# The seams between the stages of a hybrid-layer kernel, and the order inside its operand block

## What is computed

```
h = rms_norm(x) * (1 + scale) + shift                 # scale, shift, gate: silu(c) @ ada_w + ada_b
p = h @ w_in                                          # gate, u (512 each), r, k, v (512 each), lora (288)
u = silu(layer_norm(causal_conv31(u * sigmoid(gate))) * g + b)            # the conv branch
decay = exp(-exp(-softplus(-(w0 + tanh(wd) @ w2)) - 0.5));  a = sigmoid(a0 + ad @ a2)
kk = k * k_k / |k * k_k| per head;  k = k * (1 + (a - 1) * k_a)
y  = wkv7_scan(r, decay, k, v, kk, a)                 # recurrence; then norm per head, bonus, gate
x  = x + gate_m * rms_norm(concat[u, y] @ w_out)
x  = x + gate_f * rms_norm(channel_mix(h2))           # up (5632 wide), conv3, silu * value, down (2816)
for i in (0, 1):                                      # two hybrid layers
    attn, ssm = window_attention(x @ w_in_2[i]), state_space(x @ w_in_2[i])
    x = layer_norm(alpha * x + concat[attn, ssm] @ w_out_2[i]) * ln_g + ln_b
```

## Time and profile before

| | |
|---|---|
| time, median of 3 runs | 3605.99 us (3601.85 to 3607.5) |
| time of the profiled execution | 3603.5 us |
| its span, first to last instruction | 3601.4 us |
| TensorE busy | 3210.5 us (89%) |
| TensorE weight loads busy | 2560.5 us (71%) |
| VectorE, ScalarE, GpSimd busy | 1544.3, 1054.2, 1141.1 us |
| mean granted clock of TensorE | 0.938 of full speed |
| operand block | 318.5 to 424.7 us of the span |
| recurrence | 424.7 to 690.8 |
| down projection | 1329.6 to 1618.2 |
| first and second hybrid layer | 1618.2 to 2616.1, 2616.1 to 3601.4 |

### The profile page before, as it was taken

How to read it: one execution, slowest core, us unless ns; L and a number is a source line. 1 busy time by engine, 2 the same in 40 slices (tenths; PEclk the granted TensorE clock), 3 DMA queues, 4 the chain that set the end, 5 groups by cost and what they waited for, 6 DMA issues and landing times. The chain is left out here.

```text
span 3601.4 us, 49506 instructions
## 1 busy us (share of the span) xinstructions
PE 3210.5 (89%) x21000; PEld 2560.5 (71%) x21016; DVE 1544.3 (43%) x2066; ACT 1054.2 (29%) x1842; POOL 1141.1 (32%) x730
## 2 busy tenths in 40 slices
PE   6998699777999989958999998879699999988795
PEld 4885389666888878747777776768577777767684
DVE  3997644434222233341244333860312443338603
ACT  3002323323222221221244343440212443435302
POOL 2442311103333323332333332233323333323333
PEclk8998699888999999989999998989899999989898
DMA  5113300222111112113121223022131212230221
GB/s 188 52 49 98 110 4 4 68 106 62 47 52 47 47 32 97 44 73 118 47 77 59 65 82 152 1 82 97 62 82 47 79 57 65 82 152 1 97 84 64
DMA packets 211747, 254.90 MB, mean 71 GB/s; under 512 B 9408, under 2 KB 164160, under 8 KB 209120
## 3 DMA queue, kind: packets, MB, share of 16 engines
q1 hardware_dynamic: 200736, 212.21, 18.2%
q10 hardware_dynamic: 10240, 37.75, 2.7%
q0 software_dynamic: 576, 2.10, 0.1%
HBM read 203.80 MB, written 46.14 MB: 69 GB/s over the span
## 5 line engine op out<-in xcount | busy, mean ns | idle before, releaser
L1826 PE MATMUL PS<-x_high_sb,w_high_sb 128*128 128x512 f32 x1312 | 532.2, 406 | 6.4 <-POOL w_low_sb L1923 3.4
L1826 PE MATMUL PS<-x_high_sb,w_low_sb 128*128 128x512 f32 x1312 | 520.0, 396 | 0.0
L1826 PE MATMUL PS<-x_low_sb,w_high_sb 128*128 128x512 f32 x1312 | 519.5, 396 | 0.0
L1826 PEld LDWEIGHTS PS<-x_high_sb,w_high_sb 128*128 128x128 f32 x1312 | 248.3, 189 | 83.4 <-issue 23.8
L1826 PEld LDWEIGHTS PS<-x_high_sb,w_low_sb 128*128 128x128 f32 x1312 | 248.2, 189 | 58.1
L354 PE MATMUL PS<-h_high_sb,up_high_sb 128*128 128x512 f32 x704 | 274.6, 390 | 13.5 <-POOL up_low_sb L1433 13.5
L1826 PEld LDWEIGHTS PS<-x_low_sb,w_high_sb 128*128 128x128 f32 x1312 | 248.7, 190 | 52.7
L354 PE MATMUL PS<-h_low_sb,up_high_sb 128*128 128x512 f32 x704 | 274.3, 390 | 0.0
L354 PE MATMUL PS<-h_high_sb,up_low_sb 128*128 128x512 f32 x704 | 274.3, 390 | 0.0
L1483 DVE SCALAR_TENSOR_TENSOR z_sb<-PS,cols_sb,z_sb 128x1023 f32<-128x1023 f32 x88 | 112.9, 1282 | 348.1 <-ACT z_sb L1464 341.7
L1921 POOL CAST w_high_sb<-w_raw_sb 128x1024 fp32r<-128x1024 f32 x82 | 85.1, 1037 | 548.9 <-PE PS L1826 515.9
(11 more groups left out here) (397 smaller groups left out, 6468.2 us busy)
## 6 DMA issues: line engine op xcount, KB each, us to landing
w_raw_sb<-w_in SPq DMA_DIRECT2D x104, 512.0 KB, 3.8
up_raw_sb<-w_up SPq DMA_DIRECT2D x44, 512.0 KB, 3.9
ada_slots_sb<-ada_w SPq DMA_DIRECT2D x16, 1024.0 KB, 5.3
w_raw_sb<-w_out SPq DMA_DIRECT2D x64, 256.0 KB, 2.7
xbc<-staged_sb ACTq DMA_DIRECT2D x24, 512.0 KB, 2.7
down_raw_sb<-w_down SPq DMA_DIRECT2D x44, 256.0 KB, 2.6
xbc_sb<-xbc SPq DMA_DIRECT2D x2, 5376.0 KB, 19.4
attn<-HT_sb ACTq DMA_DIRECT2D x8, 1024.0 KB, 4.9
```

Source lines behind the costliest of these rows:

```text
L1826: last = pe.matmul(PS[:, bank, :], a[:, n % 2, k], b[:, k, cols], start=k == 0 and a is WH and b is HH, stop=k == KT - 1 and a is WL)
```

## The change

- In the input projection the three lora tiles come first among the others, so that tanh and sigmoid happen in mid-stage (before job 10), and the small weights of the operand block are loaded there too (`WA`, `G2`).
- The operand block: `z(0)` is TensorE's first work; three `ada` slots; decay and rate products come between the key sums; VectorE does all four `first(q)` ahead of any `second(q)`; `rk` and `decayed` move from GpSimd to VectorE, into `second(q)`; `second(q)` also takes the multiplication of the key by its norm, so `key_spread(q)` is spread over the block. The multiplication of the conv branch by its inverse deviation goes to GpSimd in the recurrence, its silus to ScalarE in the output projection, whose tiles now begin with the recurrence's.
- `down_projection` and `mix_and_norm`: five and four slots for split weights (and five for split activations of the down projection); the steps go on as before up to the last four (five), which are done token block by token block. The norm reads PSUM directly, its residual add is on VectorE, and GpSimd takes no part. The down projection sums the squares of its first half early, and copies of the first half alternate with casts for the second.
- x stays in SBUF for the first hybrid layer (no reload), the first weight tile of each hybrid layer is loaded in the stage before (`Ahead`), and the transposes of the second half of the tokens come after the first half of tile 0.

```diff
-        jobs, others = [], [("rkv", i) for i in range(3 * CT)] + [("lora", i) for i in range(3)]
+        jobs, others = [], [("lora", i) for i in range(3)] + [("rkv", i) for i in range(3 * CT)]
...
@@ mixing_operands, TensorE
+            z(0)
             for q in range(CT):
                 last = quarters(6, m.const("ones")[:, 0:32], MIX[:, q], q == 0, q == CT - 1)
             last.then_inc(s.lns, 1)
+            key_sum(0)
+            key_sum(1)
+            ada(0)
+            key_sum(2)
+            key_sum(3)
+            z(1)
+            ada(1)
             pe.wait_ge(s.lnm, 1)
+            spread(3, 0, LM, s.lnb, 1)
+            z(2)
+            ada(2)
+            z(3)
+            ada(3)
             pe.wait_ge(s.kinv, 1)
+            pe.wait_ge(s.lnc, 1)
+            key_spread(0)
+            ada(4)
+            ada(5)
+            pe.wait_ge(s.sig, 2 * CT)
+            ln_sum(0)
+            ln_sum(1)
+            ada(6)
...
             rk_sum(0)
+            key_spread(1)
+            ln_sum(2)
+            ln_sum(3)
             ada(7)
...
             last.then_inc(s.aturn, 1)
+            ada(8)
             rk_sum(1)
+            key_spread(2)
             ada(9)
+            ada(10)
             rk_sum(2)
+            key_spread(3)
             ada(11)
+            pe.wait_ge(s.lnr, 1)
+            spread(1, 0, LM, s.lnb, 3)
+            ada(12)
             rk_sum(3)
             ada(13)
...
@@ mixing_operands, VectorE, second(q)
+                v.tensor_tensor(Q(q), Q(q), pair(3), ALU.mult).then_inc(s.kkn, 1)
+                v.tensor_tensor(RKP, R(q), K(q), ALU.mult).then_inc(s.rk, 1)
+                v.scalar_tensor_tensor(out=A[:, q], in0=A[:, q], scalar=-1.0, in1=Q(q), op0=ALU.mult, op1=ALU.mult
+                                       ).then_inc(s.signed, 1)
+                v.tensor_tensor(R(q), R(q), ex2, ALU.mult)
+                v.tensor_tensor(K(q), K(q), ex1, ALU.mult)
...
@@ rwkv_recurrence, GpSimd
                     gain(k - 2)
+                    if k - 2 < CT:
+                        nc.gpsimd.tensor_tensor(MIX[:, k - 2], MIX[:, k - 2], LB[:], ALU.mult)
...
@@ down_projection, TensorE
+            for i in range(2 * FT - LAST):
                 pe.wait_ge(s.split, i + 1)
                 pe.wait_ge(s.low, i + 1)
...
+            pe.wait_ge(s.split, 2 * FT)
+            pe.wait_ge(s.low, 2 * FT)
+            for k in range(TT):
+                for i in range(2 * FT - LAST, 2 * FT):
+                    last = product(i, k)
+                last.then_inc(s.prod, 1)
...
@@ down_projection, VectorE
+                v.scalar_tensor_tensor(out=scaled[:, NH:D], in0=PS[:, k, :], scalar=rstd[:, k:k + 1],
+                                       in1=GM[:, NH:D], op0=ALU.mult, op1=ALU.mult)
+                v.scalar_tensor_tensor(out=scaled[:, 0:NH], in0=F[:, k], scalar=rstd[:, k:k + 1], in1=GM[:, 0:NH],
+                                       op0=ALU.mult, op1=ALU.mult).then_inc(s.scaled, 1)
+                v.tensor_tensor(X[:, k], X[:, k], scaled, ALU.add).then_inc(s.out, 1)
...
@@ mix_and_norm, VectorE
+                v.scalar_tensor_tensor(out=X[:, k], in0=X[:, k], scalar=minus_mean[:, k:k + 1], in1=LN[:, 0],
+                                       op0=ALU.add, op1=ALU.mult).then_inc(s.chain, 1)
+                v.scalar_tensor_tensor(out=X[:, k], in0=X[:, k], scalar=rstd[:, k:k + 1], in1=LN[:, 1],
+                                       op0=ALU.mult, op1=ALU.add).then_inc(s.out, 1)
...
@@ projections_and_attention, TensorE
-            x.tensor(pe)
             for n, job in enumerate(first):
-                half_tile(n, 0)
-                half_tile(n, 1)
+                for half in range(2):
+                    if n == 0:
+                        x.tensor(pe, half)
+                    half_tile(n, half)
```

More of the change, by code:

```diff
@@ L449, in _ @@
                 act.wait_ge(s.tile, n + 1)
+                if n == 10:
+                    for j in range(3):
+                        r = (LORA, P, GLORA - P)[j]
+                        act.wait_ge(s.shifted, shifts.index(("lora", j)) + 1)
+                        nc.scalar.activation(LO[0:r, j], LO[0:r, j], ACT.Sigmoid if j else ACT.Tanh)
                 if kind == "gate":
@@ L768, in _ @@
-            for q in range(CT):
-                v.tensor_tensor(MIX[:, q], MIX[:, q], LB[:], ALU.mult).then_inc(s.scaled, 1)
+                nc.gpsimd.tensor_tensor(MIX[:, q], MIX[:, q], LB[:], ALU.subtract).then_inc(s.centred, 1)
         @block.vector
@@ L1549, in _ @@
                 for k in range(TT):
-                    if q == 0 and half:
+                    if i == FT:
                         pe.wait_ge(s.moved, k + 1)
-                    cols = slice(k * P, (k + 1) * P)
-                    for a, b in ((MH, WH), (MH, WL), (ML, WH)):
-                        last = pe.matmul(PS[:, k, :], a[:, i % 2, cols], b[:, i % 2],
-                                         start=q == 0 and a is MH and b is WH, stop=q == FT - 1 and a is ML)
-                    if q == FT - 1:
+                    last = product(i, k)
@@ new lines, in _ @@
+            for i in range(FT):
+                high(i)
+            for k in range(TT):
+                act.wait_ge(s.prod, k + 1)
+                nc.scalar.copy(F[:, k], PS[:, k, :]).then_inc(s.moved, 1)
+                if k % 2:
+                    high(FT + k // 2)
+            for i in range(FT + TT // 2, 2 * FT):
+                high(i)
+            act.wait_ge(s.eps, 1)
+            act.wait_ge(s.moved, TT)
+            act.wait_ge(s.low, 2 * FT)
+            junk = MID[:, TT, 0:NH]
@@ L1625, in tensor @@
-    def tensor(self, pe):
+    def tensor(self, pe, half):
         m, s = self.m, self.s
-        for n in range(2 * KT):
-            half, k = n // KT, n % KT
-            if k == 0 and self.src is not None:
-                for j in range(4):
-                    pe.wait_ge(self.x_in[4 * half + j], 16)
-            if half:
-                pe.wait_ge(s.low, k + 1)
+        for n in range(half * KT, half * KT + KT):
+            k = n % KT
+            if n >= 4:
+                pe.wait_ge(s.low, n - 3)
@@ L2385, in _, with product @@
         def _(pe):
-            for i in range(2 * Q):
+            def product(i, k):
                 half, q = i // Q, tiles[i % Q]
+                high, low = weights(i)
+                for n, (a, b) in enumerate(((AH, high), (AH, low), (AL, high))):
+                    last = pe.matmul(PS[:, k, :], a[:, q, k * P:(k + 1) * P], b,
+                                     start=i % Q == 0 and n == 0, stop=i % Q == Q - 1 and n == 2)
+                return last
+            for i in range(2 * Q - LAST):
                 pe.wait_ge(s.split, i + 1)
-                if not half:
+                if i < Q:
                     pe.wait_ge(s.low, i + 1)
@@ L2394, in _ @@
                         pe.wait_ge(s.added, k + 1)
[L2395 to L2399 removed]
+                    last = product(i, k)
+                    if i == Q - 1:
                         last.then_inc(s.prod, 1)
[L2401 removed]
+                if i != Q - 1:
@@ L2402, in _ @@
                     last.then_inc(s.used, 1)
                 else:
-                    pe.wait_ge(s.prod, TT * (half + 1))
+                    pe.wait_ge(s.prod, TT)
                     pe.sem_inc(s.used, 1)
+            pe.wait_ge(s.split, 2 * Q)
+            for k in range(TT):
+                for i in range(2 * Q - LAST, 2 * Q):
+                    last = product(i, k)
+                last.then_inc(s.prod, 1)
         @block.gpsimd
         def _(pool):
-            pool.dma_start(LN[:, 0], ln_g.to_broadcast([P, D])).then_inc(s.rows_in, 16)
@@ L2424, in _ @@
+                if i >= SLOTS:
+                    pool.wait_ge(s.used, i - (SLOTS if i < Q + BACK else BACK) + 1)
+                high, low = weights(i)
+                nc.gpsimd.tensor_copy(high, RAW[:, i % 2]).then_inc(s.wchain, 1)
+                pool.wait_ge(s.wchain, i + 1)
+                nc.gpsimd.tensor_tensor(low, RAW[:, i % 2], high, ALU.subtract).then_inc(s.split, 1)
         @block.scalar
@@ L2493, in _, with first_block @@
-            centre(TT - 1)
-            normalise(TT - 2)
+            for k in range(TT):
+                add(1, k)
+                centre(k)
+                if k:
+                    normalise(k - 1)
             normalise(TT - 1)
-def first_block(m, x_mid, dst):
+def first_block(m, gate, x_mid, dst, ahead):
     nc, t = m.nc, m.t
     with ExitStack() as whole:
-        GM = alloc(m, whole, "gates", [P, 2, D])
+        GM = [gate, on_the_right(m, whole, "gate", [P, D])[:]]
         with ExitStack() as mixing:
```

567 lines of the change are left out of this document (275 added, 292 removed).

## The result

The changed kernel takes 3470.2 us (median of four runs, 3469.5 to 3471.5) against 3603.9 (3597.3 to 3607.5) for the kernel before in the same comparison: a ratio of 0.963, 95% interval 0.9615 to 0.965. The two profiled spans, 3601.4 and 3468.1, differ by 133.3 us where the sum said 110.

What follows compares the result with a forecast made beforehand. TensorE, busy 89% of the span, bounds the kernel, so time comes only from its waits. Terms -1 - 20 + 1 - 3 - 34 - 27 - 26 = -110 against the median of 3606 gave 3496 us, range 3478 to 3518.

Steps and rivals of the forecast that it cites:

- Seams: Wait at the first hybrid layer's start -34 us, end of the first layer -27, end of the second -26.
- The accumulator's output: Hybrid layers' ends: an accumulator output on VectorE costs from nothing to 0.2 us a block, 0 to +1.6 a layer.
- The rival of slow tails: Three seams: VectorE needs 4.5 us a block, not 2.75 and 3.5, giving 3526 us; chance 0.07.
- First tiles: Both hybrid layers' first tiles: overlap gains 2 to 3 us a half, clock may cost; taken 0, -6 to +10.
- The rival of the clock falling between the halves: First tiles of the hybrid layers: the clock falls between the halves, +10 us, 3506; chance 0.08.
- Operand block: Operand block from 106.2 to 85.7 us; range -11 to -30, taken -20.
- The bound of 76 to 82: Operand block at the high clock throughout: TensorE's 24.9 us would halve, VectorE's 77 with the gates being the floor.
- Down projection: Down projection before its end: +1 us at the start, -3 in the middle.
- the term of -3: Middle of the down projection: tile 22's cast follows two copies, not eight, so the 3.4 us wait goes.
- Output projection: Four silus moved into ScalarE's list there cost 0, since ScalarE has under 3 us of work per 5.4 us of products.
- Recurrence: Four branch multiplications of 2.3 us moved into GpSimd's idle time there cost 0; the recurrence keeps its 266 us.
- The rival of the GpSimd multiplications: Recurrence: each of the four multiplications delays TensorE by its whole length, +9 us, 3505; chance 0.08.

Runs made afterwards that it cites:

- experiment 8: Changed kernel with only the last step by token block at the ends of down projection and both mixings, not the last four and five: 3518.6 us, ratio 0.978.
- experiment 1: Changed kernel with all 16 groups of transposes ahead of the first tile's products again in both hybrid layers, weights still early: 3471.6 us, ratio 0.964.
- experiment 3: Changed kernel with the old first tile: transposes first through eight banks, one wait for all 16 remainders, weights still early: 3478.4 us, ratio 0.966.
- experiment 4: Kernel before with one part alone: first tile's products wait for one remainder each, transposes through four banks: 3590.9 us, ratio 0.998.
- second profile: Changed kernel, unchanged, profiled a second time: span 3469.3 us, median 3471.2, ratio 0.9635.
- experiment 9: Changed kernel with the branch's four scalings (GpSimd) and four silus (ScalarE) back at the end of the operand block: 3477.9 us, ratio 0.966.
- experiment 12: Changed kernel with the branch's four centrings moved from GpSimd to VectorE: 3468.0 us, ratio 0.963.
- experiment 10: Changed kernel with the four products of the receptance and its decay back on GpSimd: 3471.6 us, ratio 0.964.
- experiment 14: Changed kernel with a root of a constant added early in ScalarE's output projection list, so its table is in place: 3469.0 us, ratio 0.964.
- experiments 9 and 16: 16: changed kernel with root early, centrings on VectorE, key spread and sum ahead of the bias slice, fillers at four stage starts: 3454.2 us, ratio 0.959.

## Why the prediction was wrong

The direction and the mechanisms of the seams held; the size was 23 us short in the spans (26 in the medians, since the sum was set against a median 2.5 us above its own execution). Term by term:

- **Seams: right.** -34, -27, -26 against -32.8, -26.7, -26.7. A block of VectorE at the down projection's end comes every 2.78 us (2.75 in the working), in the mixings every 3.50 (3.5), and experiment 8 gave 48 us where this arithmetic asks for 49. The accumulator's output costs 0.08 us beside the sum, inside the 0 to 0.2 of the working. The rival of slow tails is refuted.
- **First tiles: the failed step, 10 us.** "... the transposes bounded the first matmul anyway (16 of 0.85 us). Turned around, each half waits for about 5.8 us and the matmuls overlap the rest: a gain of 2 to 3 us for each half. Against it, the clock ... Taken 0." The overlap gives nothing (experiment 1). And the transposes of before did not bound the first product: they end 9.4 and 9.7 us after the first, and then TensorE stands, in layer 1 for the split weights, in layer 2 for the last remainder. Waits of TensorE, before:

```profile
PE PS L1826 <- POOL w_low_sb L1923: 3.4, 1, 3.4
...
PE PS L1826 <- DVE x_low_sb L1650: 3.0, 1, 3.0
```

The gain comes from an edit that the working passed over: products wait for one remainder and no longer for all 16. Its standing time is 2.2 us a tile (experiment 3), and in the kernel before, with its four banks and nothing else of the change, it gives 2.0 to 3.2 us in layer 1 and 4.6 in layer 2 (experiment 4). What is left goes with the early weights, 2.9 us in layer 1 and 0.5 in layer 2 (experiment 1 against 4). The 11 and 13 matmuls of 0.43 us that the earlier trace rows begins are gone with it, in both layers, but why the clock fell in before and not in experiments 3 and 4 stays open. The rival of the clock falling between the halves had the sign wrong: with TensorE busy in the transposes it was at 1.00 from the first product to the last.
- **Operand block: right in its order, 5 to 6 us short.** `first` was done at 36.2 us (36.5), the bias at 54.3 (55.0), `second(2)` began at 58.8 (60.1), with a hole of 4.4 us before it (5.1), and `second(3)` ended at 75.0 (77.1). The mis-sized term is "TensorE's own list from 55.0 is 24.9 us long ... and ends at 79.9": it ends at 74.9, with VectorE, because the clock is not at 0.50 there, as in the last 25 us of before's block (its mean in the earlier trace rows is 0.61), but at 0.98, or 0.78 in the second profile, where VectorE waits 1.1 us for it. The bound of 76 to 82 for that case was given and not taken. That taking GpSimd's work from beside VectorE's makes the block shorter is shown from both sides: four scalings put back cost 7.5 us against the usual 80.9 (experiment 9), and the centrings, done by VectorE itself, give 4.4 (experiment 12). Experiment 10, with 1.9, does not stand out from the spread. What the new order of the instructions gives by itself was not tried.
- **State spaces: 6 us that the sum had no term for.** Their code is the same. Over three profiles of before they take 181.6 to 185.6, over all of after 179.6 to 181.2, and 181.1 and 180.6 in experiment 4, which has the code of before there. One profile of before can't give the size of such a stage to better than 4 us. Why the clock falls there in before and not in after stays open.
- **Down projection: -5.2 for -2.** The wait of 3.4 us is gone. Behind it six matmuls of 0.43 us for 0.23 went too, 1.2 us that the term of -3 left out. The rest is within the spread of its profiles.
- **Output projection: taken at 0, and it costs 1.3 or a little more.** "The four silus go to ScalarE's list ...: 0." Time for them there is; but they leave another function table behind, and the change back, 1.28 us, falls between the sum of squares and the root that TensorE waits for. The 1.3 us of wait are shown by experiment 14, which takes them away. The rest of the 2.4 is not: before varies from 110.5 to 111.4, after from 110.7 to 113.7 (means 110.8 and 112.4), with 13 to 25 matmuls at the low clock where before has 17 to 22.
- **Recurrence: right at 0.** The rival of the GpSimd multiplications is refuted for the place they have now (experiments 9 and 16); that they do hold VectorE beside products of SBUF tiles is experiment 9. So the Trainium skill's rule (GPSIMD Engine Reference, Key points) agrees with the trace in the block and decides nothing in the recurrence. Of the Trainium skill's other rule (ScalarE: Activation LUTs, What ACT_TABLE_LOAD costs), the 1283 ns agree with every row; the drain of about 1380 ns is in none: in after's rows under experiment 14 the root starts 1.30 us after the load does. The measurement decides.

## What to carry to other kernels

Ask of every wait that you cost what TensorE's clock does behind it: a wait of 3 us cost about 5 in before, where the clock fell behind it, and 2 in experiment 3, where it did not, and an edit that removes such a wait is worth the slow matmuls after it too. When work moves to another place in an engine's list, ask which function table it leaves behind, and who is waiting for the next function. And before a stage's size is taken from one profile, profile twice: a state space of 181 us in the program after takes up to 185.6 us in the program before and differs by 3 to 4 us between executions of that same program.

## What was not expected of the hardware

A filler matmul of 128 x 128 columns in f32 is two records and takes 0.23 us at the high clock (40 in 9.2 us), so fillers must be counted by measured length. After a wait of 3.0 to 4.2 us the clock fell in all six first tiles of before and in none of the four in experiments 3 and 4, with waits of 2.2 to 3.3 us or none: the length of the wait alone does not decide it. GpSimd's own product, 2.3 us alone, was stretched to 5.47 us when VectorE ran on (experiment 10), so the holding works both ways, and a scan is held like a product, 4.43 us for 2.28.
